# One chunk of weight sums moves from the output projection into the first mixer layer

## The reference

```python
h = h + (g_a * attn + g_c * conv) @ w_out[l]

u = _rms(h, norm_mlp[l])
h = h + jnp.square(jax.nn.relu(u @ w_mlp_in[l])) @ w_mlp_out[l]
return _rms(h, norm_final)[:, N_META:]
```

## Time and profile before

| what | value |
|---|---|
| median of 3 runs | 1282.16 us (1279.53 to 1282.68) |
| profiled execution, its own time | 1281.15 us |
| its span | 1279.1 us |
| PE busy | 1249.1 us (98%) |
| DVE busy | 813.0 us (64%) |
| ACT busy | 486.5 us (38%) |
| POOL busy | 257.0 us (20%) |
| output projection | about 699 to 773 us of the span |
| first mixer layer | about 773 to 1044 us |
| second mixer layer | about 1044 to 1256 us |

### The profile page before, as it was taken

How to read it: one execution, slowest core, us unless ns; L and a number is a source line. 1 busy time by engine, 2 the same in 40 slices (tenths; PEclk the granted TensorE clock), 3 DMA queues, 4 the chain that set the end, 5 groups by cost and what they waited for, 6 DMA issues and landing times.

```text
span 1279.1 us, 17675 instructions
## 1 busy us (share of the span) xinstructions
PE 1249.1 (98%) x7037; PEld 1086.7 (85%) x7037; DVE 813.0 (64%) x966; ACT 486.5 (38%) x731; POOL 257.0 (20%) x172
## 2 busy tenths in 40 slices
PE   6999999999999999989999989999999999999997
PEld 4888888888889999978888878888888888888886
DVE  4699999998867777764833533645111146678865
ACT  6211122532156676753621224221222244444452
POOL 2000000000034344347322322323333210000001
PEclk9999999999999999999999999999999999999999
DMA  6222222333220011114353935665312234333332
GB/s 188 67 66 66 57 67 66 104 111 107 90 66 22 22 42 33 34 30 144 100 203 109 361 141 181 237 224 201 124 55 63 66 111 149 131 126 126 131 132 98
DMA packets 136693, 142.36 MB, mean 111 GB/s; under 512 B 10573, under 2 KB 106891, under 8 KB 134586
## 3 DMA queue, kind: packets, MB, share of 16 engines
q1 hardware_dynamic: 127488, 101.55, 26.3%
q10 hardware_dynamic: 9146, 40.01, 8.2%
HBM read 115.32 MB, written 26.21 MB: 111 GB/s over the span
## 4 chain that ended last, share of the span: by engine, by line
PE 88%; DVE 4%; ACT 3%; DMA 2%; issue 2%; ACTq 1%; POOL 0%; POOLq 0%; DVEq 0%
PE psum L359 59%; PE psum L1929 17%; PE psum L1714 4%; PE psum L1746 2%; PE psum L1850 2%; DMA wst<-in_w_mlp_out 2%; PE psum L1726 1%; PE psum L1672 1%; DVE acc L1030 1%; PE psum L1590 1%; PE psum L1555 1%; DMA wsum<-wst 1%; ACT uhi L565 0%; DVE olo L1178 0%; PE psum L1857 0%
## 5 line engine op out<-in xcount | busy, mean ns | idle before, releaser
L324 POOL TENSOR_TENSOR wlo<-raw,whi 128x1024 fp32r<-128x1024 f32 (+2 forms) x70 | 166.6, 2380 | 684.1 <-ACT whi L319 684.1
L1030 DVE SCALAR_TENSOR_TENSOR acc<-cs,convw,acc 128x799 f32<-128x799 f32 x232 | 230.2, 1057 | 0.2
L319 ACT ACTIVATE whi<-raw 128x1024 fp32r<-128x1024 f32 (+1 forms) x113 | 114.0, 1009 | 294.1 <-PE psum L359 253.6
L359 PE MATMUL psum<-uhi,wlo 128*128 128x512 f32 x592 | 152.8, 339 | 0.0
L359 PE MATMUL psum<-uhi,whi 128*128 128x512 f32 x592 | 152.2, 338 | 0.5 <-DVE wlo L324 0.5
L359 PE MATMUL psum<-ulo,whi 128*128 128x512 f32 x592 | 152.5, 338 | 0.0
L1355 DVE SCALAR_TENSOR_TENSOR hid<-psum,rbc 128x768 f32<-128x768 f32 x32 | 30.6, 956 | 174.0 <-PE psum L359 173.9
L359 PE MATMUL psum<-u2hi,whi 128*128 128x512 f32 (+1 forms) x512 | 131.0, 336 | 0.0
L359 PE MATMUL psum<-u2hi,wlo 128*128 128x512 f32 (+1 forms) x512 | 130.6, 336 | 0.0
L359 PE MATMUL psum<-u2lo,whi 128*128 128x512 f32 (+1 forms) x512 | 130.6, 336 | 0.0
L916 ACT ACTIVATE hid<-hid 128x768 f32<-128x768 f32 x32 | 27.1, 846 | 200.5 <-DVE hid L1355 182.8
(11 more groups left out here) (243 smaller groups left out, 2512.7 us busy)
## 6 DMA issues: line engine op xcount, KB each, us to landing
raw<-in_w_in SPq DMA_DIRECT2D x38, 512.0 KB, 4.0
wst<-in_w_mlp_out ACTq DMA_DIRECT2D x16, 1024.0 KB, 8.0
wsum<-wst ACTq DMA_DIRECT2D x16, 1024.0 KB, 5.9
raw<-in_w_mlp_in SPq DMA_DIRECT2D x32, 512.0 KB, 4.0
raw<-wsum SPq DMA_DIRECT2D x32, 512.0 KB, 4.1
raw<-in_w_mlp_out SPq DMA_DIRECT2D x24, 512.0 KB, 3.6
gates<-gout ACTq DMA_DIRECT2D x16, 384.0 KB, 2.5
gin<-gates SPq DMA_DIRECT2D x16, 384.0 KB, 3.1
```

The source lines that it names most:

```text
L319: nc.scalar.activation(whi[:, c % 2, 0:w], raw[:, c % 4, 0:w], ACT.Copy).then_inc(hi_ready, 1)
L324: eng.tensor_tensor(out=wlo[:, c % 2, 0:w], in0=raw[:, c % 4, 0:w], in1=whi[:, c % 2, 0:w].bitcast(F32), op=ALU.subtract).then_inc(lo_read ...
L359: mm = nc.tensor.matmul(out[:, o0:o0 + n], a, b[:, k, c0:c0 + n], start=first and step == 0, stop=last and step == 2)
L1030: ins = nc.vector.scalar_tensor_tensor(out=a, in0=src, scalar=w, in1=a, op0=ALU.mult, op1=ALU.add)
```

## The change

Chunk 2 is still loaded at the same place, into slot 0. Its sums and its store are no longer in the output projection; they stand in the first mixer layer, which now has six chunks: the sums at f = 1, 3, 6, 8, 11, 13 (before: 2, 4, 6, 9, 12) and the stores at f = 2, 4, 7, 9, 12, 14 (before: 3, 5, 7, 10, 13). The chunks from 2 on alternate between slots 0 and 1. Chunk 3 alone is loaded at f = 0, and chunks 4 to 7 at f = 4, 6, 9, 11, each behind a wait for the store of chunk j-2, the last one in its slot.

```diff
-W_SLOT = (2, 0, 0, 0, 1, 0, 1, 0)
+W_SLOT = (2, 0, 0, 1, 0, 1, 0, 1)
...
             act.wait_ge(wst_stored[0], 32)
-            store_sums(2)
             u2_hi(0), u2_hi(1)
...
                     if f == 0:
-                        act.wait_ge(wst_stored[2], 32)
+                        act.wait_ge(unit_used, U_IN)
                         load_sums(3)
-                        act.wait_ge(unit_used, U_IN)
-                        load_sums(4)
-                    if f in (3, 5, 7, 10, 13):
-                        store_sums((3, 5, 7, 10, 13).index(f) + 3)
-                    if f in (4, 7, 10):
-                        j = f // 3 + 4
+                    if f in (2, 4, 7, 9, 12, 14):
+                        store_sums((2, 4, 7, 9, 12, 14).index(f) + 2)
+                    if f in (4, 6, 9, 11):
+                        j = (4, 6, 9, 11).index(f) + 4
                         act.wait_ge(wst_stored[j - 2], 32)
                         load_sums(j)
...
             h_add(0)
-            weight_sums(2)
             u2_lo(0), u2_lo(1), u2_lo(2), u2_lo(3)
...
                     if f == KH:
-                        for j in range(3, PU):
+                        for j in range(2, PU):
                             dve.wait_ge(wst_stored[j], 32)
...
-                    if f in (2, 4, 6, 9, 12):
-                        weight_sums((2, 4, 6, 9, 12).index(f) + 3)
+                    if f in (1, 3, 6, 8, 11, 13):
+                        weight_sums((1, 3, 6, 8, 11, 13).index(f) + 2)
```

## The result

The changed kernel takes 1274.47 us (median of six runs, 1273.68 to 1275.35) against 1282.42 us for the kernel before (six runs, 1279.53 to 1283.51). The ratio is 0.9941 with a 95% interval from 0.9928 to 0.9954: 0.6% faster, 7.95 us between the medians, where 5.65 were forecast. The direction and the place were right, the size was too small by 2.3 us, three tenths of what was measured.

What follows compares the result with a forecast made beforehand. PE was taken to bound the kernel, busy for 1249.1 of 1279.1 us. The terms -5.65 + 0 + 0, applied to the median of 1282.16 us, gave 1276.5 us (0.44% less), range 1273.9 to 1279.8.

Steps and rivals of the forecast that it cites:

- The stall in front of transposes 1 is all that the removal gives, and nothing takes its place: Output projection: without chunk 2's sums and store, PE's stall of 4.06 us goes whole and no other wait replaces it.
- Slack at `u2lo(0)` 1.45 us, no contention with POOL: Output projection: u2lo(0) ready at 743.84, wanted by PE at 745.29; if held until POOL's end, cost 0.07 us.
- The tail of slow clock goes with its cause: After transposes 1 start: PE at half clock from 749.35 to 752.70 loses 1.59 us, which goes with the stall.
- The size, 5.65 us: Output projection, up to transposes 2: stall of 4.06 us plus slow stretch of 1.59 us, saved together.
- The median of the runs shown lies 1.01 us above that execution, and I keep this distance: Whole kernel: the 5.65 us saved in the profiled execution (1281.15) was taken from the median, 1282.16, giving 1276.5 us.
- My rival for this point: Transposes 1: other executions stall for less than the profiled one; time 1278.1 to 1280.2 us, chance 0.15.
- The sixth chunk in the mixer costs nothing: First mixer layer, f = 1: about 7.0 us of sums fit on DVE while PE is full; cost 0.
- PE needs it only one unit later: 7 us of cover.: First mixer layer: the relu after a chunk's sums is late by less than 0.1 us, with 7 us to spare.
- ACT's tight spot, 0.67 us: Mixer steps issuing store and load together: POOL's part ends 0.67 us before PE takes it; two such places, cost 0.
- The prediction's other reading: Mixer: a store issued with a load lands at 10.4 us; load 5 waits a few tenths of a microsecond, sum unchanged.
- The slower rival: Mixer steps 6 and 11: loads 5 and 7 hold ACT, waiting for stores; up to 0.3% slower, 1286 us, chance 0.04.

Runs made afterwards that it cites:

- spread version: Kernel before, chunk 2 still in the output projection, one sum behind each of u2_lo(0) to u2_lo(3), store behind the mixer's first high weights: 1275.53 us, ratio 0.9946.
- late store: Kernel before with only the store of chunk 2 moved behind u2_hi(3) on ACT, sums unmoved on DVE: 1278.79 us, ratio 0.997.
- mixer layer with more subtractions: Changed kernel with two, four or eight more DVE subtractions behind the sums of each of chunks 2 to 7: 1274.97, 1285.18 and 1314.33 us.

## Why the prediction was right, and where it was not

- *The stall in front of transposes 1 is all that the removal gives, and nothing takes its place.* Shown. The distance is 4.75 us, and transposes 2 and 3 keep theirs. The spread version shows that it is the order in the two queues, and the late store shows that DVE's sums hold PE as well as ACT's store.
- *Slack at `u2lo(0)` 1.45 us, no contention with POOL.* `u2lo(0)` took 1.02 us from 740.74 while POOL worked from 740.00 to 742.40, and ended at 741.76, 1.6 us ahead of transposes 1. Right.
- *The tail of slow clock goes with its cause.* Right, and larger than thought: 1.59 us in the profile that I had, 1.59 to 2.93 in four.
- *The size, 5.65 us.* This is the term that was mis-sized: "Together: 755.70 - 750.05 = 5.65 us". It measures 5.65, 7.84, 8.54 and 5.69 in four profiles, 6.93 on average, against 7.05 and 7.56 us by the two ratios (0.9945 and 0.9941 of 1282). The working was exact for its execution, and that execution had one of the short stalls. The step "The median of the runs shown lies 1.01 us above that execution, and I keep this distance" carried the error into the number: I took the 1.01 us for something that stays, when part of it was the longer stall of the other runs. My rival for this point had the wrong sign; it let other executions stall for less, and no row spoke for less rather than more. That 1274.47 us still lies inside the range, 0.6 us above its lower end, is partly luck: that end came from the spread of the runs and not from a longer stall.
- *The sixth chunk in the mixer costs nothing.* Shown by leaving its sums out (253.77 against 253.76 us).
- *"PE needs it only one unit later: 7 us of cover."* Wrong. I followed the relu to PE's own wait for it and not to what stands behind it in ACT's stream. The cover is 3.0 us. The forecast didn't suffer, as the sums delay the relu by less than 0.1 us.
- *ACT's tight spot, 0.67 us.* It is there again, in steps 4 and 9. In step 4 POOL's part ends at 819.38 and PE takes it at about 820.09, when unit 5 is done: 0.7 us. Loads 5 and 7 didn't wait for their stores, which landed in 5.7 and 5.6 us (median) beside loads of 10.3 and 11.2. Each load was issued 9.3 us after the store it waits for. The prediction's other reading, that such a store lands as late as the load beside it, isn't borne out here, where both are issued on ACT's queue with the store first. The slower rival stayed away.

## What to carry to other kernels

Ask of side work not how long it is but what is queued behind it: four sums and a store cost 7 us in front of the one operation that PE wanted next, and nothing when spread between such operations or moved to a stage where PE doesn't ask. A stall that ends with a DMA has a length of its own in each execution, and one profile gives one draw; before its size goes into a forecast, hold the times of the other runs against the profiled one and let the range lean to the longer side when those are slower. And a cover ends at the first of all the chains behind the delayed operation: follow each of them through the in-order streams, not only the semaphore that PE waits for.

## What the runs showed of the hardware

Standing still for 1.99 us left PE's clock at 2.4 GHz; 3.87 to 5.46 us were each followed by a stretch at 1.2. The mixer layer with more subtractions agrees: the granted clock is 1.00 behind the three waits of 2.03 to 2.05 us, and 0.50 behind the three of 7.63 to 7.96 us. That makes the cost of a stall uneven: 2.14 us cost 0.09 more, 4.02 to 4.06 us cost 1.6 to 1.7 more, 5.41 to 5.61 us cost 2.4 to 2.9 more.

A DMA issue on ACT takes 0.9 us for two when it stands alone, and 2.3 us right behind a store:

```profile
811.90 0.81 ACTq L846 DMA_DIRECT2D wsum<-wst  x2
812.75 2.31 ACTq L841 DMA_DIRECT2D wst<-in_w_mlp_out  x2
...
821.17 0.90 ACTq L841 DMA_DIRECT2D wst<-in_w_mlp_out  x2
```

The third thing is unexplained. In the convolution's output projection, which no version touches, the steps of DVE's gated product are 8.32 us apart in some profiles and 8.48 in others, with the granted clock at 1.00 in both. The first profile of before and the second of the changed kernel:

```profile
699.31 0.96 DVE L1257 TENSOR_TENSOR gconv<-psum,gin 128x768 f32<-128x768 f32 x1 [4.50 <-PE psum L359]
```

```profile
699.59 0.96 DVE L1254 TENSOR_TENSOR gconv<-psum,gin 128x768 f32<-128x768 f32 x1 [4.66 <-PE psum L359]
```

It occurs with and without the change, and makes about 1.4 us between 632 and 691. It is part of the varying start: from the last of these steps to transposes 0 it is 41.2 or 41.3 us in all seven profiles of the two kernels.
